# A two-layer diffusion backbone step: mean squares formed ahead of the barrier, router shift transposed, modulation items reordered

## The reference, cut to what matters

```python
mod = silu(cond) @ mod_w + mod_b                    # 6 x 1024 per group
sh1, sc1, g1, sh2, sc2, g2 = split(mod, 6)
h = rms_norm(x, norm1_w) * (1 + sc1) + sh1
proj = h @ w_in                                     # Hyena, q/k/v, short conv, gates
merged = sig(ga)*(ya @ w_a) + sig(gb)*(yb @ w_b) + sig(gc)*(yc @ w_c)
x = x + g1 * (merged @ w_o)
h2 = rms_norm(x, norm2_w) * (1 + sc2) + sh2
aff = softmax(h2 @ router_w)                        # 16 experts
gate, idx = top_k(aff.T, 2*N // 16)                 # each expert takes tokens
x = x + g2 * scatter_add(gate * down(silu(h2[idx] @ w_gate) * (h2[idx] @ w_up)))
```

## Time and profile before

| | |
|---|---|
| time, median of 3 runs | 2148.35 us |
| the profiled execution's own time | 2155.39 us |
| its span | 2153.6 us |
| TensorE busy | 2095.7 us (97%) |
| VectorE busy | 1681.4 us (78%) |
| ScalarE busy | 1134.5 us (53%) |
| DMA, bytes moved | 435.80 MB, mean 202 GB/s |
| mean granted TensorE clock | 0.989 of full |
| filter stage, to the first projection | 0 to 170 us |
| expert stages | 847 to 1134 us and 1848 to 2134 us |

### The profile page before, as it was taken

One profiled execution on the slowest core, in us unless ns is written; L12 is line 12 of the kernel. 1 busy time (PEld: TensorE's weight loads), 2 busy tenths in 40 slices (PEclk: granted clock), 3 DMA queues, 4 the chain that ended last, 5 costly groups with the idle time before them and its releaser, 6 DMA issues.

```text
span 2153.6 us, 35885 instructions
## 1 busy us (share of the span) xinstructions
PE 2095.7 (97%) x13286; PEld 1707.6 (79%) x13286; DVE 1681.4 (78%) x2516; ACT 1134.5 (53%) x1798; POOL 164.2 (8%) x192
## 2 busy tenths in 40 slices
PE   8999999999999999999999999999999999999999
PEld 3449999998768997666668999999766999666666
DVE  7767878876768645999997787887777764799997
ACT  5434444324712255888884444433651225788884
POOL 1110000001001100111100000000100100111110
PEclk9999999999999999999999999999999999999999
DMA  9982433213133517999992243222413434999995
GB/s 334 329 305 87 147 136 119 83 75 117 76 118 136 171 62 294 392 382 385 382 354 98 96 147 133 98 82 76 152 42 135 159 130 159 353 378 385 385 386 216
DMA packets 76975, 435.80 MB, mean 202 GB/s; under 512 B 9228, under 2 KB 9900, under 8 KB 36381
## 3 DMA queue, kind: packets, MB, share of 16 engines
q1 hardware_dynamic: 54336, 352.87, 42.7%
q0 software_dynamic: 19024, 72.32, 10.7%
q10 hardware_dynamic: 3470, 8.64, 1.1%
HBM read 384.95 MB, written 48.84 MB: 201 GB/s over the span
## 4 chain that ended last, share of the span: by engine, by line
PE 80%; DVE 8%; ACT 4%; issue 4%; DVEq 2%; DMA 2%; ACTq 0%; POOL 0%; another core or an unknown queue 0%; POOLq 0%
PE ps L738 21%; PE ps L977 17%; PE ps L1322 9%; PE ps L1348 5%; PE ps L1326 4%; PE ps L919 3%; PE ps L1352 2%; PE ps L843 2%; PE ps L1049 2%; DMA kspec<-back 2%; PE ps L777 2%; PE ps L1174 2%; PE ps L1177 1%; PE ps L933 1%; PE ps L1102 1%
## 5 line engine op out<-in xcount | busy, mean ns | idle before, releaser
L738 PE MATMUL ps<-front_r 128*128 128x320 f32 x2432 | 417.0, 310 | 1.6 <-DVE back_r L2474 0.8
L738 PEld LDWEIGHTS ps<-front_r 128*128 128x128 f32 x2432 | 370.1, 188 | 3.0 <-DVE back_r L2474 1.4
L1420 ACT ACTIVATE front_r<-ring 128x1024 fp32r<-128x1024 f32 (+1 forms) x216 | 182.5, 845 | 261.2 <-PE ps L738 172.1
L977 PE MATMUL ps<-back_r,front_r 128*128 128x320 f32 x1728 | 265.1, 309 | 0.0
L977 PEld LDWEIGHTS ps<-back_r,front_r 128*128 128x128 f32 x1728 | 256.4, 188 | 0.0
L1420 ACT ACTIVATE back<-ps 128x512 f32<-128x512 f32 (+5 forms) x206 | 98.5, 496 | 249.6 <-PE ps L738 114.1
L977 PE MATMUL ps<-front_r 128*128 128x320 f32 x1296 | 204.7, 311 | 5.3 <-DVE back L2153 5.1
L977 PEld LDWEIGHTS ps<-front_r 128*128 128x128 f32 x1296 | 191.9, 188 | 10.4 <-DVE back L2153 9.5
L1420 ACT ACTIVATE front_r<-back 128x512 fp32r<-128x512 f32 (+2 forms) x216 | 150.1, 709 | 87.8 <-PE ps L977 35.0
L2588 DVE TENSOR_TENSOR back_r<-front,back_r 128x1024 fp32r<-128x1024 f32 x128 | 153.5, 1220 | 12.4 <-ACT back_r L1420 10.6
L1322 PE MATMUL ps<-back_r 128*80 128x512 f32 x384 | 152.3, 397 | 3.7 <-ACT back_r L1420 3.7
(11 more groups left out here) (317 smaller groups left out, 3734.8 us busy)
## 6 DMA issues: line engine op xcount, KB each, us to landing
ring<-in_stream SPq DMA_DIRECT2D x186, 1024.0 KB, 7.9
front<-in_stream SPq DMA_DIRECT2D x80, 1024.0 KB, 16.0
back<-in_stream SPq DMA_DIRECT2D x48, 1024.0 KB, 14.9
gates<-back SPq DMA_DIRECT2D x24, 640.0 KB, 3.1
back<-gates POOLq DMA_DIRECT2D x48, 320.0 KB, 3.3
kspec<-back POOLq DMA_DIRECT2D x20, 512.0 KB, 8.4
front<-kspec POOLq DMA_DIRECT2D x8, 1024.0 KB, 7.7
rows<-front ACTq DMA_DIRECT2D x10, 520.0 KB, 5.4
```

The lines of the kernel that those rows point to most:

```text
L738: mm = pe.matmul(tokh(b)[:, c0:c1], w(wp)[:, k, :], src(hp, k)[:, c0:c1], start=first, stop=last)
L977: mm = pe.matmul(ps[:, bank, 0:TH], w[:, wp, k, :], x(k), start=k == 0 and wp == 0 and x is hi and j not in (2, 6), stop=k == 3 and wp == ...
L1420: return act.activation(o, i, ACT.Copy)
```

## The change

- `LATE` becomes ((5, 6), (6, 4)), so `EARLY` is 27: two items leave the filter stage and come after the router of layer 0 (6 there, still 4 in layer 1).
- SyncE loads 3 expert items, not 6, ahead of its wait for the first gather.
- The mean squares of layer 1 and their root are formed ahead of the barrier, with 6 `keep_busy` products on constants before them.
- The router shift is done after `inverse(1)`, with one more product that turns the shift vectors (copied beforehand by ScalarE, 8 times side by side) to rows; VectorE takes the bias after L2463.
- `diag` is gone (16 ScalarE instructions per layer). In its place VectorE forms `spread_rows` (two products of 96 x 1024) in the output projection and the low part of the spread root after the affinities. `add_shift` is one fp32r product, 96 rows deep and 512 columns wide, in place of four fp32 ones.
- Three modulation items come ahead of the turn of the places, the rest after it, then 4 `keep_busy` products in layer 0 and 10 in layer 1.

```diff
-MODS, LATE = DEPTH * N_MOD, ((5, 4), (6, 4))
+MODS, LATE = DEPTH * N_MOD, ((5, 6), (6, 4))
...
                 for x in range(LAP):
-                    if x == 6:
+                    if x == 3:
...
                 if l:
-                    mean_squares(l, 0)
                     spread(l, 0)
                     keep_busy(1, 6)
...
-                        mm.then_inc(r_lg, 1)
+                        pe.wait_ge(sh_hi, 2 * l + 1)
+                        pe.matmul(ps[:, 7, 0:P], shift_cols, ident[:], start=True, stop=True).then_inc(r_lg, 1)
...
                         prompt_inverse(0)
+                        pe.wait_ge(rt_lo, 3 * l + 1)
                     forward_second()
...
                         prompt_forward()
+                    inverse(1, range(4))
+                    if o == 0:
                         router_shift()
-                    inverse(1, range(4))
...
-                    for i in range(4):
-                        mm = pe.matmul(ps[:, 4 + n % 2, P * i:P * i + P], spr[:, P * t:P * t + P],
-                                       diag[:, int(t > 0), 4 * hf + i, :], start=False, stop=i == 3)
-                    mm.then_inc(t_ready, 1)
+                    pe.matmul(ps[:, 4 + n % 2, :], spr[0:96, P * t:P * t + P],
+                              spread_rows[0:96, int(t > 0), 4 * hf:4 * hf + 4, :].rearrange("p i n -> p (i n)"),
+                              start=False, stop=True).then_inc(t_ready, 1)
...
-                for i in mods:
+                for x, i in enumerate(mods):
+                    if x == 3:
+                        turn_places()
                     mod_rows(i)
-                    if i > mods[0]:
+                    if x:
                         mod_columns(i - 1)
                 mod_columns(mods[-1])
+                keep_busy(2, 10 if l else 4)
...
+                if l + 1 < DEPTH:
+                    pe.wait_ge(c_read, l * 8 + 6)
+                    keep_busy(2, 6)
+                    pe.wait_ge(c_read, l * 8 + KC)
+                    mean_squares(l + 1, 0)
                 end_phase(pe, l)
...
-                if l:
-                    root(l, 0)
                 norm(l, 0 if l else 4, KC)
...
+                        act.wait_ge(r_lg, 2 * l + 1)
+                        copy(shift_rows, ps[:, 7, 0:P]).then_inc(sh_hi, 1)
                         act.wait_ge(y_sum, l * 4 + 1)
...
+                    if o == 0:
+                        act.wait_ge(modcol_read, conv_mods(l, o)[-1] + 1)
+                        copy(shift_cols.rearrange("p (j m) -> p j m", j=8), mod[:, l, 24:32, :].rearrange("p k g -> p (k g)")
+                             .unsqueeze(1).to_broadcast([P, 8, 16])).then_inc(sh_hi, 1)
...
-                        act.activation(diag[:, g, k, :], ident[:], ACT.Identity, scale=mod[:, l, 24 + k, g:g + 1])
...
                         square(2 * l + 2, m)
+                    root(l + 1, 0)
                 end_phase(act, l)
...
+                    if c == 3:
+                        whole = [96, KC, P]
+                        for g in range(2):
+                            ins = dve.tensor_tensor(spread_rows[0:96, g], shift_rows[0:96, :].bitcast(F32).unsqueeze(1).to_broadcast(whole),
+                                                    sel16[0:96, g:16:2].unsqueeze(2).to_broadcast(whole), ALU.mult)
+                        ins.then_inc(rt_lo, 1)
...
+                dve.wait_ge(z_ready, l * Z_IN + Z_IN)
+                dve.tensor_tensor(spr[32:64, :], spread_at(l, 1)[32:64, :], spr[32:64, :].bitcast(F32),
+                                  ALU.subtract).then_inc(rt_lo, 1)
                 dve.wait_ge(r_affT, l + 1)
```

More of the change, by code:

```diff
@@ L156, in build @@
             pass
+        with nc.sbuf_tensor("shift_rows", [P, QK], F32R) as shift_place:
+            pass
+        shift_rows = shift_place[:, P:2 * P]
         qkw = sb("qkw", [P, QK])
+        shift_cols = qkw[:, 2 * P:3 * P]
         cs = sb("cs", [P, KC, 32])
@@ L263, in build @@
         sgin, mtmp = region(106, [4, T]), region(116, [2, T])
-        z, spr, diag = region(56, [KC, T]), region(86, [T]), region(76, [2, KC, P])
+        z, spr, spread_rows = region(56, [KC, T]), region_r(86, [T]), region_r(76, [2, KC, P])
         rws, lbias = region(139.5, [2, KC, 2 * NE]), qkw[:, 0:NT * NE].rearrange("p (t e) -> p t e", t=NT)
@@ L350, in build @@
         scattered, yo_free, acc_in, e_xt = sem("scattered"), sem("yo_free"), sem("acc_loaded"), sem("e_xt")
-        e_up, e_silu, e_hid, e_t, e_hidT, e_yev, e_ycev = (sem(n) for n in (
-            "e_up", "e_silu", "e_hid", "e_t", "e_hidT", "e_yev", "e_ycev"))
+        sh_hi, rt_lo = sem("shift_rows_hi"), sem("shift_and_root_lo")
+        e_silu, e_hid, e_t, e_hidT, e_yev, e_ycev = (sem(n) for n in (
+            "e_silu", "e_hid", "e_t", "e_hidT", "e_yev", "e_ycev"))
         e_xhi, e_xlo = sem("e_x_hi"), sem("e_x_lo")
@@ L1158, in router_shift @@
                             for k in range(KC):
-                                mm = pe.matmul(ps[:, 7, 320 + NE * g:320 + NE * g + NE],
+                                pe.matmul(ps[:, 7, 320 + NE * g:320 + NE * g + NE],
                                                mod[:, l, 24 + k, g:g + 1].to_broadcast([P, P]), rw[:, k, :],
                                                start=k == 0, stop=k == KC - 1)
-                        mm.then_inc(r_lg, 1)
+                        pe.wait_ge(sh_hi, 2 * l + 1)
+                        pe.matmul(ps[:, 7, 0:P], shift_cols, ident[:], start=True, stop=True).then_inc(r_lg, 1)
                     def inverse(kt, tiles):
@@ L1284, in _, with turn_places @@
                     add_shift(n)
[L1286 to L1294, removed]
+                def turn_places():
+                    pe.wait_ge(r_places, l * 2 + 1)
+                    apart(pe)
+                    pe.transpose(ps[0:SLOTS, 0, 0:LISTS], places[:], ident[0:LISTS, 0:LISTS])
+                    pe.transpose(ps[0:CAP[1], 0, LISTS:2 * LISTS], best[:], ident[0:LISTS, 0:LISTS]).then_inc(r_placesT, 1)
+                    pe.wait_ge(numbers_in, l * 32 + 32)
+                    pe.wait_ge(r_places, l * 2 + 2)
+                    apart(pe)
+                    seconds = turned[0:CAP[1], :].rearrange("p (a n) -> p a n", a=2)[:, :, 32:32 + NE]
+                    pe.matmul(ps[0:CAP[1], 1, 0:2 * NE], flip, seconds, start=True, stop=True).then_inc(r_placesT, 1)
                 mods = late_mods(l, 1)
-                for i in mods:
+                for x, i in enumerate(mods):
+                    if x == 3:
+                        turn_places()
                     mod_rows(i)
-                    if i > mods[0]:
+                    if x:
                         mod_columns(i - 1)
                 mod_columns(mods[-1])
+                keep_busy(2, 10 if l else 4)
                 def turn_rows(ee, n):
@@ L2454, in _ @@
                         branch_lo(0)
[L2455 to L2459, removed]
                     for m in range(4):
@@ L2467, in _ @@
                         ins.then_inc(y_out, 1)
+                    if o == 0:
+                        dve.wait_ge(r_lg, 2 * l + 1)
+                        dve.wait_ge(sh_hi, 2 * l + 2)
+                        for g, t0, t1 in ((0, 0, 1), (1, 1, NT)):
+                            dve.tensor_copy(lbias[:, t0:t1, :], ps[:, 7, 320 + NE * g:320 + NE * g + NE].unsqueeze(1)
+                                            .to_broadcast([P, t1 - t0, NE]))
+                        dve.tensor_tensor(shift_rows[64:96, :], ps[64:96, 7, 0:P], shift_rows[64:96, :].bitcast(F32),
+                                          ALU.subtract).then_inc(rt_lo, 1)
                 dve.wait_ge(y_inv, l * 10 + 10)
```

5 lines of the change are left out of this document (3 added, 2 removed).

## The result

| | before | after |
|---|---|---|
| median of 15 runs, us | 2149.45 | 2157.85 |
| lowest to highest, us | 2146.66 to 2151.87 | 2151.29 to 2164.09 |
| ratio, with its 95% interval | | 1.0038 [1.0028, 1.0049] |
| profiled execution: own time / span, us | 2155.39 / 2153.6 | 2162.92 / 2161.1 |

The changed kernel is slower by 0.38%, some 8 us; forecast were 4.7 us less, and a range that ended at 2151.5. Its runs also spread over 13 us, against 5 before.

What follows compares the result with a forecast made beforehand. TensorE was taken as the bound (97% busy), with DMA also at its limit in the expert stage. Terms -3.5 + 1.3 + 1.8 - 3.0 - 1.3 = -4.7 us gave a median of 2143.7 us, range 2137.5 to 2151.5.

Steps and rivals of the forecast that it cites:

- What bounds the kernel: Whole kernel: TensorE busy 97%; in the expert stage DMA and TensorE are both at their limit, the later end holds.
- Filter stage, -3.5: Filter stage: two modulation items and their 2 MB load fewer save 3.5 us, within bounds of 1.4 and 5.8.
- Router shift, +1.3: Shift moved behind inverse(1): a 0.7 us gap and one added product cost 0.65 us a layer, 1.3 in all.
- Router stage, gather 2.3 earlier: Router stage: one-matmul add_shift and earlier places move the gather from 843.24 to 840.9 us, 2.3 earlier.
- Start of the experts, -2.4 and -3.4: TensorE's side of the expert stage: 2.6 us from a higher clock, giving -2.4 in layer 0 and -3.4 in layer 1.
- The stream's side, +1.8 and -3.0: Expert weight loads: later loads less the margin make the stage end +1.8 us in layer 0, -3.0 in layer 1.
- The margin of 8.1: Weight stream: last load lands 6.6 us before ScalarE takes it, plus 1.5 made up between ScalarE and TensorE.
- Barrier, -1.3: Barrier before layer 1: root formed earlier and spread at full clock save 1.3 us, bounds 0.5 and 2.
- The 2.7 that would come with a drain: Barrier: the skill's page puts a 1.38 us drain on the table load; by its figures the part would be -2.7.
- number 2: Rival: stream's margin overdrawn in both layers, layer 0 +8.2, layer 1 +2.3; in all +9.2, 2157.5 us; chance 0.11.
- The test that I set: Layer 0's expert stage: forecast wrong if it is shorter from gather to end, or its stalls exceed 6 us.

Runs made afterwards that it cites:

- Run 12: Kernel before with the barrier part and one item moved from the filter stage into layer 0's convolution (LATE ((6, 4), (6, 4))): 2147.25 us, ratio 0.9983.
- run 8: Kernel before with the barrier part alone (mean squares, root and six keep_busy products ahead of the barrier): 2148.14 us, ratio 0.9992.
- Run 2: Changed kernel with LATE ((5, 4), (6, 4)) again, still three loads ahead of the gather: 2154.45 us, ratio 1.0014 to the kernel before.
- run 3: Changed kernel with both stream edits taken back (six loads ahead, LATE ((5, 4), (6, 4))): 2151.33 us, ratio 1.0004 to the kernel before.
- Run 9: Kernel before with no expert load, instead of six, ahead of the wait for the first gather: 2170.75 us, ratio 1.0099.
- run 4: Kernel before with only three expert loads, instead of six, ahead of the wait for the first gather: 2155.73 us, ratio 1.0028.
- run 6: Run 3's kernel with the router shift again ahead of inverse(1): 2148.34 us, ratio 0.9991 to the kernel before.
- run 1: Changed kernel with six expert loads ahead of the first gather again, late items as changed: 2157.58 us, ratio 1.0025 to the kernel before.
- run 10: Run 6's kernel with one item moved from the filter stage into layer 0's convolution: 2148.67 us, ratio 0.9987 to the kernel before.
- run 7: Run 3's kernel with the turn of the places ahead of all late items: 2163.35 us, ratio 1.0052 to the kernel before.
- run 5: Run 3's kernel without the keep_busy products ahead of the turn of the gathered rows: 2151.30 us, ratio 1.0002 to the kernel before.

## Why the prediction was wrong

- **What bounds the kernel**: right, and it was the warning. "Both are at their limit, so the stage has two ends, and the later one holds" is what happened.
- **Filter stage, -3.5**: not shown. The 4.6 of the two profiles lies within the 6 us over which the start of the first projection moves between profiles of equal code. Run 12 against run 8 has one item less there and one more in the convolution: 0.09%, 1.9 us lower, which is not clear of noise.
- **Router shift, +1.3**: 0.8 and 1.1, so 1.9; right in mechanism, half as large again. The gap is 0.3 larger in layer 1.
- **Router stage, gather 2.3 earlier**: 2.1 in layer 0, against 0.5 *later* in layer 1, where the items in front of the places fell to the lower clock. Run 2 has the same two cases the other way round (24.6 in layer 0, 22.0 in layer 1). And it holds only with three loads ahead; with six the rows' stores release the gather. The prediction gave the last store 4.5 us to that point, and in run 3 it takes 8.5.
- **Start of the experts, -2.4 and -3.4**: wrong. The clock gave 1.5, not 2.6. The layer 0 items, costed at 1.67 us, ran at 2.8, and the `keep_busy` products, costed at 0.43, at 0.94: both were priced at the full clock. In layer 0 TensorE turned the rows 5.5 us later than before, so its own end would be some 4.4 later (with the 290.2 us that the stage takes in run 3, not 291.3). The stream's end there is 7.0 later, and the later holds.
- **The stream's side, +1.8 and -3.0**: this is the step that failed. The margin of 8.1 (6.6 past ScalarE and 1.5 "made up between ScalarE and TensorE") isn't there. Run 9 puts 14.8 us of lateness in front and loses 9.3 and 9.5; run 4 puts 7.4 and loses 2.1 and 4.1. That is 3.3 to 5.5 of margin. In layer 1 of the kernel before, the loads went out 1.2 us ahead of TensorE's turn of the rows (1846.76 and 1848.00), and in runs 4 and 9 together with it; with that counted it is 4.5 to 6.5. Past the margin a load costs 2.4 us in layer 0 and 1.8 in layer 1 (run 9 less run 4 is 7.1 and 5.4 for three), near the 2.5 taken. Stage and router together are +7.0 in layer 0 and +2.8 in layer 1, 11 us worse than forecast, and this carries the sign. About half of it is the margin, 2 to 3 us in each layer. The other half is when the loads behind the gather could start, some 3 us in each: in layer 0 the gather's landing was taken as 6 us and was 8.7, and in layer 1 it went out 0.5 later instead of 2.3 earlier.
- **Barrier, -1.3**: right: 1.4 by run 8's timeline and 1.7 by its time, 2.0 in the profile of the changed kernel, of which 1.1 is the clock of the spread. The 2.7 that would come with a drain did not show.
- **Rivals**: number 2 is what came, +9.2 forecast and +8.2 measured, at a chance of 0.11. "It decides from the point where loads are over 6.6 us later" was near to the truth: run 4, at 7.4, is over it and slower. It gave +8.2 for layer 0 and +2.3 for layer 1; measured are 7.0 and 2.8. Its price came out near by terms that are partly others, and so in part by luck: 1.8 to 2.4 per load past the margin and not 2.95, a smaller margin, and in layer 0 a late landing. What it said against itself, that the loads run at 426 GB/s in the first stretch, was worth little, since the stage is bound by its mean, 382 to 385.
- The test that I set, "the forecast is wrong if its stalls exceed 6 us", was no good one: ScalarE's waits for loads are 3.6 us in layer 0 and 5.0 in layer 1, less than the loss. The waits hide in TensorE's and VectorE's own; the chain of waits shows them, the total doesn't.

Put together from the ratios: barrier -1.7 (run 8); shift +1.9 to +2.8 (run 6); three loads +2.2 (run 2 less run 3); two items moved from the filter stage into layer 0's queue +4.5, what the filter stage gives for them included (run 1 less run 3); fast `add_shift`, item order and `keep_busy` +0.9 (run 10 less run 12), which is not distinct from 0. The sum is 7.8 to 8.7, and +8.2 was measured. Each of these terms has an error of 2 to 4 us, so the agreement is better than it had to be. The three loads cost 6.0 on the kernel before and 2.2 on run 3; at that error the two can't be told apart. The gather would explain a difference in layer 1 only (22.0 in run 2, 23.7 in run 3); in layer 0 it is 1.0 later in run 2.

Left open: how much of the two items' 4.5 us is their place in SyncE's queue and how much the gather that lands beside the late loads, for no run has the one without the other. Also why the runs of the changed kernel spread over 13 us and those of run 7 over 18. Both have items behind the places at the lower clock, and the stretches at the lower clock lie elsewhere in each profile, but no run tested it. The low part of the root and `spread_rows` were not run by themselves.

## What to carry to other kernels

Where a stage has its DMA share at 1.0, its prefetch margin is a stock that every turn draws on: read the latency of the loads by turn, and where it grows, every load fewer at the start costs, once the margin is gone, about its transfer at the end (2.4 and 1.8 us here). Don't add to the margin that the last load shows what two engines "could make up": here it was 4.5 to 6.5 where the last load showed 6.6 and 8.1 was taken. And when an edit moves work into a wait, price that work at the clock that it will itself leave, and look in every queue (SyncE's here) for what is now issued behind it.

## What the runs showed of the hardware

- The first gather of a stage, a third of a megabyte, lands in 3.8 to 5.0 us in the layers where the loads ahead of it are in (4.0 and 4.5 in run 9, which has none ahead), and in 8.6 and 8.7 where they are not (layer 0 of run 1 and of the changed kernel). It is not held up by all that is queued: between 1080 and 1120 us of the changed kernel a gather lands in 10.1 us and loads in 24.7 to 27.0. The Trainium skill (DMA: Bandwidth & Descriptors, Queues, rings and completion order) has the queues take turns by packets; the trace agrees so far as the gather passes loads that were asked for before it.
- Of a stage's first microseconds at the lower clock less is lost than the clock would say. In layer 1 of run 5 the rows are turned at 1841.3 and the clock rises at 1849.4; in run 3 the experts' start is at 1.00. Eight microseconds at half speed would be 4 lost, and the stages differ by 1.2 (291.4 and 290.2). TensorE is busy for only 6.23 of these 8.1 us and ScalarE for 6.69 (in layer 0, 5.97 of 6), so it was not TensorE alone that set the pace; that it was ScalarE's copies is argued, not shown.
- At a granted clock of 0.50 TensorE was busy for 15.94 of 20 us with 95 matmuls (run 7). A high busy share in such a row is no sign of much work: the matmuls are only longer.
